# A 64x64 recurrence on all four quadrants of TensorE with its steps at listed places, and a state-space stage with fewer opening loads and weight pieces rounded by ScalarE

## The reference

```python
def wkv7_scan(r, decay, k, v, kk, a):          # 8 heads of 64, over 1024 tokens
    def step(S, inp):
        r_t, w_t, k_t, v_t, kk_t, a_t = inp
        s_kk = jnp.einsum('bhij,bhj->bhi', S, kk_t)
        S = (S * w_t[:, :, None, :] - s_kk[..., None] * (a_t * kk_t)[:, :, None, :]
             + v_t[..., None] * k_t[:, :, None, :])
        return S, jnp.einsum('bhij,bhj->bhi', S, r_t)
    ...
def hybrid_layer(...):                          # twice
    ...
    attn = sliding_window_attention(q, k, v, sinks) * jax.nn.silu(z_attn)
    y = ssd_chunked(xs, dt, a, bm, cm)          # 8 chunks of 128 tokens
    ...
    out = jnp.einsum("ble,ed->bld", jnp.concatenate([attn, ssm], axis=-1), w_out)
    return layer_norm_2(DEEPNORM_ALPHA * x + out, ln_g, ln_b)
```

## Time and profile before

| | us |
|---|---|
| median of 3 runs | 3308.29 |
| the profiled execution, its own time | 3310.31 |
| span of the trace | 3308.5 |
| TensorE busy | 3067.4 (93%) |
| VectorE busy | 1553.2 (47%) |
| ScalarE busy | 1104.1 (33%) |
| GpSimd busy | 985.4 (30%) |

### The profile page before, as it was taken

How to read it: one execution, slowest core, us unless ns; L and a number is a source line. 1 busy time by engine, 2 the same in 40 slices (tenths; PEclk the granted TensorE clock), 3 DMA queues, 4 the chain that set the end, 5 groups by cost and what they waited for, 6 DMA issues and landing times. The chain is left out here.

```text
span 3308.5 us, 50039 instructions
## 1 busy us (share of the span) xinstructions
PE 3067.4 (93%) x21074; PEld 2427.3 (73%) x21074; DVE 1553.2 (47%) x2316; ACT 1104.1 (33%) x1885; POOL 985.4 (30%) x638
## 2 busy tenths in 40 slices
PE   5999799795999998998999999889889999998898
PEld 3887489674888887887877777667678777776676
DVE  3999745434223233335024433378441334434775
ACT  3012333233212222123134444465222344445532
POOL 2442022202323333332233333232223333331421
PEclk8999899897999999999999999999999999999999
DMA  5112400032111111122212122666541122127754
GB/s 204 48 51 71 166 4 4 22 120 96 45 51 47 48 51 42 48 99 93 67 49 77 64 64 99 200 202 169 155 120 52 39 76 83 52 96 254 208 155 140
DMA packets 342537, 308.57 MB, mean 93 GB/s; under 512 B 11424, under 2 KB 300576, under 8 KB 337856
## 3 DMA queue, kind: packets, MB, share of 16 engines
q1 hardware_dynamic: 269088, 243.67, 23.7%
q10 hardware_dynamic: 73248, 62.00, 5.9%
HBM read 248.89 MB, written 54.66 MB: 92 GB/s over the span
## 5 line engine op out<-in xcount | busy, mean ns | idle before, releaser
L1914 PE MATMUL PS<-x_high_sb,w_high_sb 128*128 128x512 f32 x1312 | 530.1, 404 | 0.0
L1914 PE MATMUL PS<-x_high_sb,w_low_sb 128*128 128x512 f32 x1312 | 518.2, 395 | 0.0
L1914 PE MATMUL PS<-x_low_sb,w_high_sb 128*128 128x512 f32 x1312 | 517.4, 394 | 0.0
L1914 PEld LDWEIGHTS PS<-x_high_sb,w_high_sb 128*128 128x128 f32 x1312 | 246.9, 188 | 76.1 <-issue 23.9
L1914 PEld LDWEIGHTS PS<-x_high_sb,w_low_sb 128*128 128x128 f32 x1312 | 246.8, 188 | 57.9
L360 PE MATMUL PS<-h_high_sb,up_high_sb 128*128 128x512 f32 x704 | 274.9, 390 | 13.5 <-POOL up_low_sb L1436 13.5
L1914 PEld LDWEIGHTS PS<-x_low_sb,w_high_sb 128*128 128x128 f32 x1312 | 247.3, 188 | 52.4
L1493 DVE SCALAR_TENSOR_TENSOR z_sb<-PS,cols_sb,z_sb 128x1023 f32<-128x1023 f32 x88 | 112.8, 1282 | 348.8 <-ACT z_sb L1474 342.4
L2398 PE MATMUL PS<-w_high_sb,attn_high_sb 128*128 128x512 f32 x512 | 224.2, 438 | 56.4 <-POOL w_low_sb L2516 32.0
L360 PE MATMUL PS<-h_low_sb,up_high_sb 128*128 128x512 f32 x704 | 274.6, 390 | 0.0
L360 PE MATMUL PS<-h_high_sb,up_low_sb 128*128 128x512 f32 x704 | 274.6, 390 | 0.0
(11 more groups left out here) (419 smaller groups left out, 6014.1 us busy)
## 6 DMA issues: line engine op xcount, KB each, us to landing
xbc_sb<-w_in SPq DMA_DIRECT2D x80, 512.0 KB, 3.8
up_raw_sb<-w_up SPq DMA_DIRECT2D x44, 512.0 KB, 3.9
ada_slots_sb<-ada_w SPq DMA_DIRECT2D x16, 1024.0 KB, 7.1
decays_sb<-running_sums SPq DMA_DIRECT2D x16, 1024.0 KB, 7.1
attn_raw_sb<-state_out ACTq DMA_DIRECT2D x32, 512.0 KB, 4.5
attn_raw_sb<-attn ACTq DMA_DIRECT2D x30, 512.0 KB, 4.6
xbc<-staged_sb ACTq DMA_DIRECT2D x24, 512.0 KB, 2.7
xbc_sb<-xbc SPq DMA_DIRECT2D x16, 768.0 KB, 8.2
```

The costliest lines, as they stand in the source:

```text
L1914: last = pe.matmul(PS[:, bank, :], a[:, n % 2, k], b[:, k, cols], start=k == 0 and a is WH and b is HH, stop=k == KT - 1 and a is WL)
```

## The change

In the recurrence nine steps go from `by_chunk` to a new `by_quarter` that takes a matmul's rows, its buffers' indices and its output from three maps, so that four matmuls in a row fall in four quadrants: AP1, SQ2a, SQ2b, AP2, SQ3, GV, FR, FF and Z. Their outputs take two banks where they took one (Z had two). AP1 and AP2 are no longer "inverse plus product", added by VectorE on the way out, but a product with power plus identity, which VectorE writes as a second move of SQ1a and SQ2a into the buffer `PI`. PB and N write their odd heads crosswise. The four 64x64 matmuls for the output that followed S0 in one quadrant (L1079) go behind S1, which now has eight in two quadrants. GV's two ScalarE copies of 128 partitions become four of 64. The table holds a place for each step in place of a cost.

In the state-space stage the load of the attention rows of unit 1 moves from ScalarE's opening to SyncE at the end of the stage before. SyncE's opening is reordered, with two waits on the loads of units 2 and 3. At the end of chunks 2 and 6 it issues four weight pieces ahead of the store and the gate load. Rounding of pieces 9 to 31 goes from GpSimd to ScalarE (`cast`).

```diff
-        steps = [("PB", 2, "dve", 1.2), ("N", 2, "dve", 0.6), ("TRa", 2, "act", 1.8), ("SQ1a", 1, "dve", 1.0),
...
-        whole = sum(cost for *_, cost in steps)
+        steps = [("PB", 2, "dve", 0.0), ("N", 2, "dve", 0.1), ("TRb", 2, "act", 4.2), ("SQ1a", 1, "dve", 5.2),
...
+        whole = 54.2
+        choice = {2: ((0, 1), (2, 3)), 1: ((0,), (1,), (2,), (3,))}
...
+        quarters = [(f, par, c) for f in range(CT) for par in range(2) for c in range(2)]
+        plain = lambda f, par, c: (half(c), CT * par + f)
+        first = lambda f, par, c: (half(c ^ par), CT * par + f)
+        home = lambda f, par, c: (half(c), CT * (c ^ par) + f)
+        away = lambda f, par, c: (half(c ^ par), CT * c + f)
...
+            def by_quarter(bank, left, left_at, right, right_at, out_at, width=CH, stop=True, check=False):
+                for f, par, c in quarters:
+                    (rows, i), (_, j), (out, n) = left_at(f, par, c), right_at(f, par, c), out_at(f, par, c)
+                    at = n % CT * width
+                    last = pe.matmul(PS[out, bank + n // CT, at:at + width], left[rows, i], right[rows, j],
+                                     start=width == CH or f == 0, stop=stop, skip_group_check=check)
+                return last
...
+                elif name == "PB":
+                    for f, par, c in quarters:
+                        left, right = A[feat(par), f, chunk(c)], RKQ[feat(par), f:f + 2 * CT + 1:2 * CT, chunk(c)]
+                        if par == 0:
+                            pe.matmul(PS[half(c), b0, f * P:(f + 1) * P].rearrange("p (a n) -> p a n", a=2), left, right,
+                                      start=True, stop=True)
+                        else:
+                            pe.matmul(PS[half(c), b0 + 1, f * P:f * P + CH], left, right[:, 0], start=True, stop=True)
+                            last = pe.matmul(PS[half(1 - c), b0 + 1, f * P + CH:(f + 1) * P], left, right[:, 1],
+                                             start=True, stop=True)
...
                 elif name == "SQ2b":
-                    last = by_chunk(b0, PW2[:, g, 0], PW2[:, g, 1])
+                    empty(pe, (k, g, "SQ1a"))
+                    empty(pe, (k, g, "SQ1b"))
+                    last = by_quarter(b0, PW2[:, g, 0], first, PW2[:, g, 1], first, home)
...
                 elif name == "AP2":
                     empty(pe, (k, g, "SQ2a"))
                     empty(pe, (k, g, "AP1"))
-                    last = by_chunk(b0, PW4[:, g, 0], IB[:, g])
+                    last = by_quarter(b0, PI[:, g], home, IB[:, g], home, away)
...
                 elif name == "Z":
+                    empty(pe, (k, g, "AP3"))
                     empty(pe, (k, g, "GV"))
-                    last = by_chunk(b0, IB[:, g], XR[:, g], P, True, False, True)
+                    last = by_quarter(b0, IB[:, g], away, XR[:, g], away, home, P, False, True)
...
-                    for f in range(CT):
-                        last = pe.matmul(PS[half(c), 4 * g + 2, hcol(2 * f + c)], RKQ[feat(c), f, chunk(c)],
-                                         state(k, c)[feat(c), f], start=False, stop=True, skip_group_check=True)
+                    for f, d in [(f, d) for f in range(CT) for d in range(2)] if c else []:
+                        last = pe.matmul(PS[half(d), 4 * g + 2, hcol(2 * f + d)], RKQ[feat(d), f, chunk(d)],
+                                         state(k, d)[feat(d), f], start=False, stop=True, skip_group_check=True)
...
-                elif name in ("SQ1a", "SQ2a"):
-                    ins = v.tensor_copy(flat((PW2 if name == "SQ1a" else PW4)[:, g, 0]), B)
-                elif name in ("AP1", "AP2", "AP3"):
+                elif name == "SQ1a":
+                    v.tensor_copy(flat(PW2[:, g, 0]), B)
+                    ins = v.tensor_tensor(PI[:, g], by_head(B), ident_rows, ALU.add)
+                elif name == "SQ2a":
+                    v.tensor_copy(slots(PW4[:, g, 0]), two)
+                    ins = v.tensor_tensor(slots(PI[:, g]), two, ident_of, ALU.add)
+                elif name in ("AP1", "AP2"):
+                    ins = v.tensor_copy(slots(IB[:, g]), two)
+                elif name == "AP3":
                     ins = v.tensor_tensor(flat(IB[:, g]), flat(IB[:, g]), B, ALU.add)
...
             first_weights(3)
+            sp.wait_ge(s.biased, N)
+            sp.dma_start(land.AA[:, 1], attn_d[:, :, P:2 * P].rearrange("k p t -> p k t")).then_inc(land.aa_in[1], 16)
...
             rows(0)
+            residual(0)
             sp.dma_start(skip, d_skip.to_broadcast([P, SH])).then_inc(s.skip_in, 16)
-            residual(0)
+            sp.wait_ge(aa_in[0], 32)
             rows(1)
             residual(1)
             rate_rows(1)
             for signal, count in gates_stored:
                 sp.wait_ge(signal, count)
+            gates(0)
+            sp.wait_ge(aa_in[1], 32)
+            rows(2)
             for i in range(KT, KT + 4):
                 weights(i)
-            rows(2)
-            gates(0)
             sp.wait_ge(land.rest_stored, 16)
             residual(2)
...
+                at = {0: KT + 4, 2: WS + 4, 6: WS + KT + 4}.get(c)
+                for i in range(at, at + 4) if c in (2, 6) else ():
+                    weights(i)
                 if c:
                     store(c - 1)
                 if c + 1 < TT:
                     gates(c + 1)
-                for i in {0: range(KT + 4, WS + 4), 2: range(WS + 4, WS + KT + 4),
-                          6: range(WS + KT + 4, WS + 2 * KT + 4)}.get(c, ()):
+                for i in range(at + 4, at + KT) if c in (2, 6) else range(at, WS + 4) if c == 0 else ():
                     weights(i)
...
+            def cast(i):
+                act.wait_ge(raw_in[i % 4], 16 * (i // 4 - KT // 4 + 1))
+                slot_empty(act, i)
+                nc.scalar.copy(WH[:, i % WS], RAW[:, i % 4]).then_inc(s.wcast, 1)
...
             high(0)
-            load(1)
...
+                if c in (2, 6):
+                    at = WS if c == 2 else WS + KT
+                    for i in range(at, at + KT):
+                        cast(i)
...
                 high(u)
+                if u == UNITS - TT:
+                    for i in range(WS + 2 * KT, 4 * KT):
+                        cast(i)
```

More of the change, by code:

```diff
@@ L918, in rwkv_recurrence @@
             joins = name in ("H1", "H2", "S0", "S1", "YX", "Y")
-            before[key] = [] if joins else sorted({last_in[b] for b in banks if b in last_in})
+            before[key] = [] if joins else sorted({last_in[b] for b in own if b in last_in})
             if eng is not None:
-                for b in banks:
+                for b in own:
                     last_in[b] = key
@@ L957, in _ @@
                     empty(pe, other)
-                b0 = banks[0]
+                b0 = own[0]
                 cols = unit_cols(k)
@@ L986, in _ @@
                 elif name == "SQ1a":
+                    empty(pe, (k, g, "PB"))
                     empty(pe, (k, g, "N"))
@@ L1002, in _ @@
                     empty(pe, (k, g, "TRa"))
-                    for f, par, i, h in every:
-                        for c in range(2):
-                            last = pe.matmul(PS[half(c), b0, i * CH:(i + 1) * CH], GR[half(c), g, i, 1],
-                                             v[half(c), hcol(h)], start=True, stop=True)
+                    for f, par, c in quarters:
+                        (rows, i), (out, n) = plain(f, par, c), away(f, par, c)
+                        at = n % CT * CH
+                        last = pe.matmul(PS[out, b0 + n // CT, at:at + CH], GR[rows, g, i, 1], v[rows, hcol(2 * f + par)],
+                                         start=True, stop=True)
                 elif name == "AP2":
@@ L1054, in _ @@
                                       v[half(c), hcol(h)], start=f == 0, stop=False, skip_group_check=True)
-                    for f, par, i, h in every:
-                        for c in range(2):
-                            pe.matmul(PS[feat(par), b0 + c, f * HD:(f + 1) * HD], nb[half(c), hcol(h)],
-                                      WU[half(c), g, i, HD:P], start=False, stop=False, skip_group_check=True)
+                    for f, par, c in quarters:
+                        rows, i = home(f, par, c)
+                        pe.matmul(PS[feat(par), b0 + c, f * HD:(f + 1) * HD], nb[rows, hcol(2 * f + par)],
+                                  WU[rows, g, i, HD:P], start=False, stop=False, skip_group_check=True)
                     for f, par, i, h in every:
@@ L1062, in _ @@
                                       start=h == 0, stop=False, skip_group_check=True)
-                    for f, par, i, h in every:
-                        for c in range(2):
-                            last = pe.matmul(PS[half(c), b0 + 2, hcol(h)], BR[half(c), g, i, 0], WU[half(c), g, i, HD:P],
-                                             start=False, stop=False, skip_group_check=True)
```

(12 more changed lines are left out.)

130 lines of the change are left out of this document (71 added, 59 removed), and 13 rows, old and new, of the table steps.

## The result

The changed kernel takes 3264.8 us (median of 4 runs) against 3306.5 for the kernel before on the same chip: a ratio of 0.9874, 95% interval 0.9854 to 0.9894. The forecast was 3222, range 3198 to 3257. The sign was right; half of the gain did not come. The profiled execution took 3262.0 us with a span of 3260.2, 48.3 less than the span before.

A forecast was written before the change was run, and what follows sets the result against it. It took TensorE's own steps to bound the recurrence, and waits on loads and weight pieces to lengthen the state-space stages. Savings of 38 + 49 = 87 us off 3310.3 gave 3223, 3222 as median; range 3198 to 3257.

The forecast's parts named there:

- signs of being wrong: Forecast counts as wrong if recurrence units stand over 28 us apart, or either state-space stage is under 15 us shorter.
- Price of the steps: Recurrence: four quadrants save 0.44 us on each of eight 64-wide steps and 0.77 on Z; VectorE near 132 us busy.
- I take 38, which the matmul rows give: Recurrence: shorter TensorE steps give back 4.75 us a unit, 38 us over eight units; bounds 28 to 42.
- Rival B: Recurrence bound by its moves, fixed order leaves gaps: gain 28 us or less, down to 14; 3233 to 3247; chance 0.15.
- Its rule from the Trainium skill: Recurrence: when small tiles speed up TensorE, emptying PSUM may become the bound; VectorE's 16.5 us in 25.85 spoke against.
- The rule weighed and set aside: Recurrence: matmul starts never under about 25 ns apart; per record a four-quadrant step takes 0.80 us, saving 14 us in all.
- I take 2160, 8 us saved, and 6 in the second layer: State-space opening: wait for chunk 2's inputs ends at 2160, not 2168.08; 14 us saved over both layers.
- lower bound of 3 each: State-space opening: least saving per layer, 3 us, if the transfer wins everything but what was moved out.
- Rival A: State-space stages: waits only move, to transfers or ScalarE's list; stages give only 20 us, 3252 in all; chance 0.13.
- Crossing 7 to 8: State-space, between unit groups: earlier weight pieces save 6 us a layer, 12 in all, after 6.5 us of new waits.
- The later crossings: State-space crossings 15 to 16 and 23 to 24: 7 and 4.5 us saved a layer, 14 and 9 in all.
- Half of the spread of the stages: State-space stages: saving taken as 35 to 62 us in the forecast's own bounds, 3206 to 3247; full bounds 20 to 72.

The follow-up runs named there:

- e1: Only the recurrence part of the change, put in the kernel before: 3293.9 us, ratio 0.9954 to the kernel before.
- e5b: Changed kernel with another table of places, wide steps laid between dense four-quadrant ones, AP1 kept ahead of SQ2a: 3252.2 us, ratio 0.9832 to the kernel before.
- e2: Only the state-space part of the change, put in the kernel before: 3283.7 us, ratio 0.9925 to the kernel before.
- e7: Changed kernel with eight more FF in a row per unit, the added ones 32 columns wide instead of 64: 3322.9 us, ratio 1.0048 to the kernel before.
- s1: Changed kernel with the last 2 MB of the residual issued behind chunk 2's inputs: 3256.4 us, ratio 0.9833 to the kernel before.
- s4: Changed kernel with chunk 2's inputs issued first, then chunk 3's decay rows, then the last residual: 3247.1 us, ratio 0.9823 to the kernel before.
- s3: Changed kernel with weight pieces rounded on GpSimd as before, four early loads kept: 3273.9 us, ratio 0.9894 to the kernel before.
- e4: Changed kernel with FF issued nine times in a row per unit instead of once: 3321.2 us, ratio 1.0034 to the kernel before.
- e3: Changed kernel with SQ2a, SQ2b, AP2 and SQ3 issued two quadrants at a time: ratio 0.9870 to the kernel before.
- e6: Changed kernel with nine FF in a row per unit, issued two quadrants at a time: 3325.3 us, ratio 1.0055 to the kernel before.

## Why the prediction was wrong

Both of its signs of being wrong came: units stand 29.3 us apart, not under 28, and the second layer's stage is 9.0 us shorter, not 15 (304.6 to 295.6; the first one's 21.3). Of the 87 us forecast, 38 were the recurrence's and 14 the openings'; these two terms failed.

- *Price of the steps: right.* 0.43 to 0.47 us a step for 0.44, 0.86 for Z where 0.77 were taken, and VectorE at 135 us busy where 132 were forecast.
- *"I take 38, which the matmul rows give": the step that failed first.* It measured 14.1 us in the two traces, 15 by e1. The sum took TensorE's steps and the moves as the only limits, and the supply of instructions at nothing. Before, a unit's 856 records took 30.6 us, 4.6 us for 128 of them (a block of 256 instructions) in the mean, and its pauses summed to 0.2 us. The forecast unit has 872 records in 25.85 us, 3.8 us a block in the mean and less in its dense stretches, where the trace after has work of 2.6 to 3.5 us in a block and the blocks come 3.5 to 4.3 us apart. 20.9 us of pauses and the 14.1 gained make 35 of the 38. Rival B gave 14 to 28 and named the moves; the size fits, the cause does not (e5b), so that it came close is luck. Its rule from the Trainium skill, on emptying PSUM (TensorEngine Tiling (Array Packing), PSUM Bottleneck), is not borne out here: VectorE stays at 135 of 257 us.
- *The rule weighed and set aside.* By the Trainium skill (TensorE: Matmul & The Clock Gate, Part 1) 25 ns a record would have made the gain 14 us, which is what came. That too is chance: on four quadrants records start every 15 to 16 ns (476.24 to 477.20), and order alone took the pauses away (e5b).
- *"I take 2160, 8 us saved, and 6 in the second layer": the second step that failed.* 2.4 and 0.1 us in the two traces. Over the eight traces that have the changed stages whole (changed kernel, e2 to e7 with e5b) an opening takes 45.2 and 45.3 us in the mean, in the two with the stages of before (before, e1) 46.8 and 46.6. The sum put 12.75 MB ahead of chunk 2's inputs at 0.333 MB/us, 38 us. Its megabytes were of 1024 KB, 13.4 of those in which the rate is given, so the same sum makes 40; and the window has 318 GB/s over 46 us, 14.6 MB. The lower bound of 3 each was near it. Rival A was right here: the wait only moved. The change had not moved the inputs ahead of anything; s1 and s4 did.
- *Crossing 7 to 8: right in size.* 6.4 and 4.6 us (34.9 to 28.5, 32.5 to 27.9) for 6 each, with the 2 us wait that was forecast. What s3 shows was missed: the gain is the early loads', and the rounding on ScalarE takes some of it back. (The inputs late by 4.58 us in the earlier trace rows are chunk 5's, not chunk 4's.)
- *The later crossings: right.* From the end of that crossing (2246.74 in the earlier trace rows) to the stage's end 182.6 to 170.9 us in the first layer and 184.4 to 175.0 in the second, 21.1 for 23; half of it is the loads' (s3). One wait for a piece of 2.3 us is left in the second layer, where none over 1 was forecast.
- *The range.* Half of the spread of the stages is 35 to 60.5, not 62; that moves the forecast's bound of 3206 by 1 us and nothing else.
- *Open.* The stretch from chunk 2's inputs to the crossing took 42.0 us in the second layer before and 47.1 after, a loss of 5; in the first layer 43.8 and 42.9. Most of both is spread between executions: the eight traces named above have 42.9 to 45.4 and 43.5 to 47.1, in the mean 44.6 and 45.1, the two with the stages of before 42.7 and 43.3 in the mean. A loss of about 2 us a layer remains, as much as the opening gains. No run singles out a part of the change for it.

Sum of the traces: 14.1 + 2.5 (opening) - 4.2 (the stretch behind it: 0.9 won, 5.1 lost) + 11.0 + 21.1 = 44.5 of the 48.3; the rest lies in places that the change does not touch.

## What to carry to other kernels

When steps of few columns get faster, count instructions as well as columns. Here, where 128 matmul records with their weight loads (a block of 256 instructions) were quicker than about 4 us, one block after another, TensorE paused for its own instructions. Steps with few instructions (wide matmuls, transposes) belong between such steps, not behind them. A load that is moved out of a full stretch helps only if what is needed next moves forward in the queue: take the bytes ahead of the next operand, not the wait that is seen first. Here order alone took 8 us a layer off the opening (45.6 to 37.4 and 37.0), and order is free.

## What the runs showed of the hardware

- TensorE's instructions come in packets of 16 KB, 256 instructions (55 packets for 54.4 blocks). Dense blocks in a row were seen 3.5 to 4.3 us apart (518.31 less 514.59 in e4; 475.90, 480.21, 484.36 after). The pauses stand under "issue" in the profile, inside steps, 256 instructions or a multiple from each other within one.
- A single block of 2.29 us behind one of 5.00 passed without a pause (489.36 after).
- A four-quadrant matmul record of 32 columns starts no faster than one of 64: 17 ns (e7, 477.21), 16 ns (e4, 514.59).
- The same two quadrants at a time cost 0.62 to 0.7 us a step when the order alternates four quadrants in pairs (e3, e6), and 0.94 in `by_chunk`.
